# Delta rule on one NeuronCore: the order in which TensorE takes the heads of both parities

## The chip, the cores and the metric

The kernel runs on one core of one Trainium2 chip. The metric is the device time of one execution in microseconds; the median of several runs counts. A profile of one execution gives every instruction's start and length on each engine: TensorE (PE, with its weight loads as PEld), VectorE (DVE), ScalarE (ACT), GpSimd (POOL) and the queue of SyncE that issues transfers (SPq).

## What is computed

The reference is a network of four layers over 256 tokens of width 1024, batch 1. The change concerns one mixer of the third layer, RWKV-7 time mixing, which is a delta rule with 8 heads of dimension 64:

```python
def step(state, inp):                       # state: per head 64 x 64
    r_t, w_t, k_t, v_t, kk_t, b_t = inp
    sa = jnp.einsum('bhvk,bhk->bhv', state, -kk_t)
    state = (state * w_t[:, :, None, :] + sa[..., None] * b_t[:, :, None, :]
             + v_t[..., None] * k_t[:, :, None, :])
    return state, jnp.einsum('bhvk,bhk->bhv', state, r_t)
_, y = lax.scan(step, state0, xs)           # over 256 tokens
...
y = ((y - mu) * lax.rsqrt(var + RW_GN_EPS)).reshape(b, s, c) * lnx_g + lnx_b
y = (y + bonus.reshape(b, s, c)) * g
```

Behind it come the output projection of this layer, its feed-forward part, and a fourth layer with a mixture of experts, which takes the second half of the time.

## The kernel before

**Tiling.** The 256 tokens are taken in two halves of 128 (`tt` = 0, 1), and each half in four chunks of 32 (`cc`, `CH`). The eight heads are four pairs `j`; the head `h = 2j + odd` has parity `odd`. In tensors that lie by feature, an even head has partitions 0 to 63 and an odd one 64 to 127 (`rows_of`), so these are also the rows of TensorE's array that it uses; where the output goes to `rows_of(h)`, the parity also sets the half of the array's columns. All of it is fp32, and PE runs each such product as two instructions, all at the one line of the helper `mm` (L476).

**The stage, on PE** (`delta_pe`, once for each half): transposes to token order (L2123); for each head the products `mp` (L2131, L2132), which VectorE masks (L2288); the lower triangles `low` (L2134 to L2141), four heads of one parity into one PSUM bank, masked by VectorE at L2294; warm-ups (`keep_warm`: products on constants whose result nobody reads); five levels of powers of a triangular inverse; the products NV, WT (L2187, heads in turn) and Z. Then for each chunk: the products `u` with the state (L2201 to L2211), one warm-up ahead of them and one behind, the sums on VectorE (L2327, one for each parity), the products `s` of the new state (L2216 to L2220, heads in turn), and the state's update on VectorE (L2335, L2340). Last the outputs `y` (L2225 to L2239): for each parity a bank, and in it for each head one product with `u`, one with the values (both over 128 tokens into 64 columns), and four with the chunks' states (64 rows into 64 columns).

**Beside it.** `beside(i)` places steps of another attention (MLA) between these, on all engines, and for i = 13 to 17 the normalisation of the first half's y: mean, variance, and `finish_dve` with `affine_act` (L2443 to L2450 on VectorE, L2463 on ScalarE), which stand ahead of the second half's copies in each engine's order.

**What comes behind.** ScalarE copies y from its two banks (L2268), once for each parity; in the first half the token copies (L2247) and the masks of the next half (L2288) wait for the last y. In the second half PE goes on with the output projection (`out_pe`): it first takes the parts that do not need y (k = 4 to 7), with the mean of y behind the first of them (`rest_of_delta`, `mean_pe`), the variance later, and then the parts that need the finished y (L2454 on VectorE). The state products of a half end with the marker that lets `finish_dve` of the first half run.

**Order.** Each engine runs its own list in order, and semaphores join them. PSUM has eight banks, six of which (`short`) are used here in turn; `bank_free` waits for the release of the bank's user six openings before. The weights stream through a ring of slots; SyncE issues a slot's transfers when its last user is done. In this stage no slot comes free and next to nothing is transferred.

Of the kernel before, what the change touches and what calls it, by code (L numbers as in the profile page):

```python
# [23 lines left out]
P = 128  # L24
# [4 lines left out]
HD = 64  # L29
# [15 lines left out]
CH = 32  # L45
# [429 lines left out]
def mm(pe, out, lhsT, rhs, start=True, stop=True):  # L475
    return pe.matmul(out, lhsT, rhs, start=start, stop=stop)  # L476
# [3 lines left out]
def warm(g, pe, ps, count):  # L480

    for _ in range(count):
        mm(pe, ps[:, 0:SHARED], g.tab("mean"), g.tabs[:, 0:SHARED])


def keep_warm(g, pe, count):


    pe.wait_ge(*g.bank_free())
    warm(g, pe, g.psum[g.next_bank("short")], count)  # L490
# [1614 lines left out]
def rows_of(h):  # L2105
    return slice(HD * (h % 2), HD * (h % 2) + HD)


def delta_pe(g, pe, tt, beside):

    pe.wait_ge(g.s["dve_delta"], g.at("A~"))
    pe.wait_ge(g.s["dve_delta"], g.at("shifted", 11))
    pe.wait_ge(g.s["dve_delta"], g.at("B~"))
    pe.wait_ge(g.s["dve_delta"], g.at("K~"))
    pe.wait_ge(g.s["dve_delta"], g.at("R~"))
    pe.wait_ge(g.s["dve_delta"], g.at("chunk ends"))
    c = slice(P * tt, P * tt + P)
    src = [g.ar[:, :, tt, 0, :], g.bt[:, :, c], g.kt[:, :, c], g.prj[:, 8:12, 1 + P * tt:1 + P * tt + P]]
    for n, s in enumerate(src):
        pe.wait_ge(*g.bank_free())  # L2120
        ps = g.open(("tok", tt, n))
        for j in range(4):
            last = pe.transpose(ps[:, P * j:P * j + P], s[:, j, :], g.tab("ident"))  # L2123
        last.then_inc(g.s["pe_delta"], 1)
        g.count("pe_delta", ("mm", "tok", tt, n))
    for h in range(8):
        r, j = rows_of(h), h // 2
        pe.wait_ge(*g.bank_free())
        ps = g.open(("mp", tt, h))
        both = g.ar[r, j, tt, :, :].rearrange("p w c -> p (w c)")  # L2130
        mm(pe, ps[:, 0:256], g.bt[r, j, c], both)  # L2131
        mm(pe, ps[:, 256:512], g.kt[r, j, c], both).then_inc(g.s["pe_delta"], 1)  # L2132
        g.count("pe_delta", ("mm", "mp", tt, h))
    for odd in range(2):  # L2134
        pe.wait_ge(*g.bank_free())
        ps = g.open(("low", tt, odd))
        for j in range(4):
            r = rows_of(odd)
            last = mm(pe, ps[:, P * j:P * j + P], g.ar[r, j, tt, 0, :], g.bt[r, j, c])
        last.then_inc(g.s["pe_delta"], 1)  # L2140
        g.count("pe_delta", ("mm", "low", tt, odd))  # L2141

    keep_warm(g, pe, 4)
    for lv in range(5):
        pe.wait_ge(g.s["dve_delta"], g.at("F", tt, lv, 0))
        pe.wait_ge(g.s["dve_delta"], g.at("F", tt, lv, 1))
        pe.wait_ge(g.s["dve_delta"], g.at("powers", tt, lv, 0))
        pe.wait_ge(g.s["dve_delta"], g.at("powers", tt, lv, 1))
        pe.wait_ge(*g.moment(("lows", tt, lv, 0)))
        pe.wait_ge(*g.moment(("lows", tt, lv, 1)))  # L2150
        for odd in range(2):
            heads = [2 * j + odd for j in range(4)]
            if lv < 4:
                pe.wait_ge(*g.bank_free())
                ps = g.open(("D", tt, lv, odd))
                for j, h in enumerate(heads):
                    last = mm(pe, ps[:, P * j:P * j + P], g.mp[:, h, 0, :], g.dm[:, h, :])
                last.then_inc(g.s["pe_delta"], 1)
                g.count("pe_delta", ("mm", "D", tt, lv, odd))
            if lv < 3:  # L2160
                pe.wait_ge(*g.bank_free())
                ps = g.open(("U", tt, lv, odd))
                for j, h in enumerate(heads):
                    last = mm(pe, ps[:, P * j:P * j + P], g.dm[:, h, :], g.mp[:, h, 0, :])
                last.then_inc(g.s["pe_delta"], 1)
                g.count("pe_delta", ("mm", "U", tt, lv, odd))
            if lv > 0:
                pe.wait_ge(*g.bank_free())
                ps = g.open(("Fp", tt, lv, odd))
                for j, h in enumerate(heads):  # L2170
                    last = mm(pe, ps[:, P * j:P * j + P], g.dm[:, h, :], g.fm[:, h, :])
                last.then_inc(g.s["pe_delta"], 1)
                g.count("pe_delta", ("mm", "Fp", tt, lv, odd))
            g.also("pe_delta", ("read", tt, lv, odd))
        beside(9 * tt + lv)
    pe.wait_ge(g.s["dve_delta"], g.at("F", tt, 5, 0))
    pe.wait_ge(g.s["dve_delta"], g.at("F", tt, 5, 1))
    pe.wait_ge(*g.bank_free())
    ps = g.open(("NV", tt))
    for h in range(8):  # L2180
        last = mm(pe, ps[:, HD * h:HD * h + HD], g.mp[:, h, 2, :], g.tok[:, 3, HD * h:HD * h + HD])
    last.then_inc(g.s["pe_delta"], 1)
    g.count("pe_delta", ("mm", "NV", tt))
    pe.wait_ge(*g.bank_free())
    ps = g.open(("WT", tt))
    for h in range(8):
        last = mm(pe, ps[rows_of(h), P * (h // 2):P * (h // 2) + P], g.tok[:, 0, HD * h:HD * h + HD], g.fm[:, h, :])  # L2187
    last.then_inc(g.s["pe_delta"], 1)
    g.count("pe_delta", ("mm", "WT", tt))
    pe.wait_ge(g.s["act_delta"], g.at("nv", tt))  # L2190
    pe.wait_ge(*g.bank_free())
    ps = g.open(("Z", tt))
    for h in range(8):
        last = mm(pe, ps[:, HD * h:HD * h + HD], g.fm[:, h, :], g.nv[:, HD * h:HD * h + HD])
    last.then_inc(g.s["pe_delta"], 1)
    g.count("pe_delta", ("mm", "Z", tt))
    pe.wait_ge(g.s["act_delta"], g.at("wt", tt))
    for cc in range(4):
        n = 4 * tt + cc
        q = slice(CH * cc, CH * cc + CH)  # L2200
        for odd in range(2):  # L2201
            pe.wait_ge(*g.bank_free())
            ps = g.open(("u", n, odd))
            if odd == 0:
                warm(g, pe, ps, 1)
                pe.wait_ge(g.s["dve_delta"], g.at("state", n))
            for j in range(4):
                last = mm(pe, ps[q, HD * j:HD * j + HD], g.wt[rows_of(odd), j, q],
                          g.states[rows_of(odd), n % 5, HD * j:HD * j + HD])
            last.then_inc(g.s["pe_delta"], 1)  # L2210
            g.count("pe_delta", ("mm", "u", n, odd))  # L2211
        pe.wait_ge(*g.bank_free())
        ps = g.open(("s", n))
        warm(g, pe, ps, 1)
        pe.wait_ge(g.s["dve_delta"], g.at("U row", n))
        for h in range(8):  # L2216
            o = ps[rows_of(h), HD * (h // 2):HD * (h // 2) + HD]
            v = slice(HD * h, HD * h + HD)
            mm(pe, o, g.tok[q, 2, v], g.tok[q, 3, v], True, False)
            last = mm(pe, o, g.tok[q, 1, v], g.u[q, v], False, True)  # L2220
        last.then_inc(g.s["pe_delta"], 1)
        g.count("pe_delta", ("mm", "s", n))
        beside(9 * tt + 5 + cc)

    for odd in range(2):  # L2225
        r = rows_of(odd)
        pe.wait_ge(*g.bank_free())
        ps = g.open(("y", tt, odd))
        for j in range(4):
            h = 2 * j + odd  # L2230
            v, o = slice(HD * h, HD * h + HD), slice(P * j, P * j + P)
            mm(pe, ps[r, o], g.u[:, v], g.mp[:, h, 1, :], True, False)
            mm(pe, ps[r, o], g.tok[:, 3, v], g.mp[:, h, 3, :], False, False)
            for cc in range(4):
                o = slice(P * j + CH * cc, P * j + CH * cc + CH)
                last = mm(pe, ps[r, o], g.states[r, (4 * tt + cc) % 5, HD * j:HD * j + HD],
                          g.ar[r, j, tt, 1, CH * cc:CH * cc + CH], False, cc == 3)
        last.then_inc(g.s["pe_delta"], 1)
        g.count("pe_delta", ("mm", "y", tt, odd))  # L2239


def delta_act(g, act, tt, beside):
# [989 lines left out]
def second_block(g, kind, e):  # L3232
# [18 lines left out]
    for t in range(2):  # L3251
        only("pe", delta_pe, t, beside)
        only("act", delta_act, t, beside)
        only("dve", delta_dve, t, beside)
# [326 lines left out]
```

## Time and profile before

| | |
|---|---|
| median of 3 runs | 2783.79 us (2780.58 to 2784.04) |
| the profiled execution | 2780.89 us, span 2779.1 us, mean granted clock 0.981 |
| PE busy | 2663.9 us, 96% |
| VectorE / ScalarE busy | 1818.8 us, 65% / 1458.3 us, 52% |
| the delta rule | about 1201 to 1357 us of the span |
| y of each half | 1268.6 to 1277.8, 1347.9 to 1357.2 |

The span runs from the first to the last instruction; the execution is 1.8 us longer. A row of the timeline merges neighbours of one kind: it has the start of the first, the time to the end of the last, and the count. Matmuls overlap in the pipeline, so one lasts longer than the distance to the next, and from the length of a group of n the tail of one is taken off before it is divided. "128\*64 128x128" is the part of the array that a matmul uses (rows by columns) and the tile it writes. The clock's column PEclk is 1.00 for 2.4 GHz and 0.50 for 1.2 GHz.

### The profile page before, as it was taken

The page shows a single profiled execution, that of the slowest core. Times are in us where ns is not written, and L with a number is a line of the kernel's source. Part 1 is how long each engine was busy: PE and PEld are TensorE (multiplying, and loading weights), DVE is VectorE, ACT ScalarE, POOL GpSimd, SP SyncE. Part 2 cuts the span into 40 slices and gives each one's busy share as a digit, 9 for nine tenths or more (in the row PEclk, how much of TensorE's full clock was granted, in tenths as well). Part 3 has the DMA queues.
Part 4 walks back from the last instruction along what each step waited for, and adds up shares of the span by engine and source line. Part 5 has one row for each costly group of instructions (what it writes and reads, how often), then busy time and mean ns, then how long its engine had stood idle before and what let it go on. Part 6 is the DMA issues. An engine that isn't in the chain of part 4 may idle for free.

```text
span 2779.1 us, 39065 instructions
## 1 busy us (share of the span) xinstructions
PE 2663.9 (96%) x15510; PEld 2246.9 (81%) x15510; DVE 1818.8 (65%) x1912; ACT 1458.3 (52%) x1624; POOL 29.5 (1%) x40
## 2 busy tenths in 40 slices
PE   6999989999898999899999998899999999999999
PEld 4775678888796999877799996788888888888887
DVE  4224675553534786774454544788888888888887
ACT  3226343342325565522244343677777777777776
POOL 0002000000002000000000000000000000000000
PEclk9999999999999999999999999899999999999999
DMA  8456422222230445320144440799999999999996
GB/s 348 166 213 243 152 91 91 91 107 83 105 131 34 187 173 187 118 92 1 37 174 156 171 182 14 270 365 346 365 341 344 372 346 364 348 369 346 357 360 259
DMA packets 84360, 590.45 MB, mean 212 GB/s; under 512 B 9616, under 2 KB 10000, under 8 KB 19472
## 3 DMA queue, kind: packets, MB, share of 16 engines
q1 hardware_dynamic: 82800, 576.79, 55.6%
q10 hardware_dynamic: 1440, 11.93, 1.1%
q8 instruction: 91, 1.49, 0.2%
q14 instruction: 29, 0.24, 0.0%
HBM read 587.63 MB, written 1.05 MB: 212 GB/s over the span
## 4 chain that ended last, share of the span: by engine, by line
PE 90%; DVE 5%; ACT 3%; issue 1%; DMA 1%; DVEq 0%; POOL 0%; ACTq 0%; POOLq 0%; SPq 0%
PE banks L470 24%; PE banks L472 24%; PE banks L471 24%; PE banks L476 16%; PE banks L2894 1%; PE banks L925 1%; DMA hT<-in_h 1%; DVE rstd L830 0%; DVE ring_rounded L545 0%; DVE aT L2288 0%; ACT scratch L1002 0%; DVE activations L1445 0%; DMA ring<-in_stream 0%; ACT scratch L1015 0%; DVE scratch L2075 0%
## 5 line engine op out<-in xcount | busy, mean ns | idle before, releaser
L471 PE MATMUL banks<-ring_rounded,activations_rounded 128*128 128x512 f32 x1344 | 523.2, 389 | 0.0
L471 PE MATMUL banks<-aT_rounded,ring_rounded 128*128 128x256 f32 (+1 forms) x1096 | 355.8, 325 | 0.0
L472 PE MATMUL banks<-aT_rounded,ring_rounded 128*128 128x256 f32 (+2 forms) x1120 | 336.0, 300 | 0.0
L545 DVE TENSOR_TENSOR ring_rounded<-ring,ring_rounded 128x2048 fp32r<-128x2048 f32 (+4 forms) x112 | 225.4, 2018 | 161.2 <-ACT ring_rounded L535 160.3
L471 PEld LDWEIGHTS banks<-ring_rounded,activations_rounded 128*128 128x128 f32 x1344 | 252.7, 188 | 50.2
L3068 DVE TENSOR_TENSOR ring_rounded<-ring,tables_rounded 128x2048 fp32r<-128x2048 f32 x112 | 253.6, 2288 | 24.1 <-ACT tables_rounded L2986 23.4
L3068 DVE TENSOR_TENSOR ring_rounded<-ring,aT_rounded 128x2048 fp32r<-128x2048 f32 x112 | 254.5, 2286 | 14.5 <-ACT aT_rounded L2986 13.6
L2986 ACT ACTIVATE tables_rounded<-ring 128x2048 fp32r<-128x2048 f32 x112 | 215.0, 1920 | 87.6 <-DMA ring<-in_stream 81.6
L535 ACT ACTIVATE ring_rounded<-ring 128x2048 fp32r<-128x2048 f32 (+4 forms) x112 | 188.5, 1690 | 133.0 <-PE banks L472 99.9
L2986 ACT ACTIVATE aT_rounded<-ring 128x2048 fp32r<-128x2048 f32 x112 | 215.0, 1920 | 71.2 <-DMA ring<-in_stream 58.8
L470 PE MATMUL banks<-aT_rounded,ring_rounded 128*128 128x256 f32 (+1 forms) x776 | 235.0, 303 | 16.6 <-DVE aT_rounded L855 12.5
L472 PE MATMUL banks<-activations_rounded,ring_rounded 128*128 128x512 f32 (+1 forms) x724 | 244.9, 338 | 0.0
L471 PEld LDWEIGHTS banks<-aT_rounded,ring_rounded 128*128 128x128 f32 x1096 | 213.8, 195 | 15.2 <-issue 0.5
L472 PEld LDWEIGHTS banks<-aT_rounded,ring_rounded 128*128 128x128 f32 (+1 forms) x1120 | 218.2, 195 | 5.7
L545 DVE TENSOR_TENSOR ring_rounded<-ring,third_upper_rounded 128x2048 fp32r<-128x2048 f32 (+3 forms) x56 | 113.7, 2030 | 101.1 <-ACT third_upper_rounded L535 100.7
L470 PE MATMUL banks<-tables_rounded,activations_rounded 128*128 128x512 f32 x448 | 176.7, 394 | 0.0
L470 PE MATMUL banks<-aT_rounded,activations_rounded 128*128 128x512 f32 x448 | 176.0, 393 | 0.0
L472 PE MATMUL banks<-tables_rounded,activations_rounded 128*128 128x512 f32 x448 | 174.6, 390 | 0.0
L472 PE MATMUL banks<-aT_rounded,activations_rounded 128*128 128x512 f32 x448 | 174.6, 390 | 0.0
L471 PE MATMUL banks<-aT_rounded,third_upper_rounded 128*128 128x256 f32 (+1 forms) x536 | 173.9, 324 | 0.0
L470 PEld LDWEIGHTS banks<-aT_rounded,ring_rounded 128*128 128x128 f32 x776 | 152.7, 197 | 22.5 <-issue 18.8
L470 PE MATMUL banks<-activations_rounded,ring_rounded 128*128 128x512 f32 (+1 forms) x464 | 157.8, 340 | 0.0
(353 smaller groups left out, 5534.8 us busy)
## 6 DMA issues: line engine op xcount, KB each, us to landing
ring<-in_stream SPq DMA_DIRECT2D x501, 1024.0 KB, 5.5
ring<-in_stream SPq DMA_DIRECT2D x32, 704.0 KB, 5.1
ring<-in_stream SPq DMA_DIRECT2D x28, 768.0 KB, 6.0
activations<-in_rpb ACTq DMA_DIRECT2D x2, 1536.0 KB, 6.2
ring<-in_stream SPq DMA_DIRECT2D x6, 512.0 KB, 5.0
tables<-in_tab_b ACTq DMA_DIRECT2D x1, 2436.0 KB, 8.8
tables<-in_tab_a ACTq DMA_DIRECT2D x1, 2304.0 KB, 13.1
hT<-in_h ACTq DMA_DIRECT2D x1, 2048.0 KB, 15.8
```

Of the source, the lines that this page charges most:

```text
L470: pe.matmul(out, exact(upper), exact(w_upper), start=start, stop=False)
L471: pe.matmul(out, exact(upper), exact(w_lower), start=False, stop=False)
L472: return pe.matmul(out, exact(lower), exact(w_upper), start=False, stop=stop)
L476: return pe.matmul(out, lhsT, rhs, start=start, stop=stop)
L535: act.activation(exact(upper), w, ACT.Copy).then_inc(g.s["act_pieces"], 1)
L545: dve.tensor_tensor(exact(w), w, rounded(upper), ALU.subtract).then_inc(g.s["dve_pieces"], 1)
L925: last = pe.transpose(ps[:, o * w + P * t:o * w + P * t + P], probs[:, j % 2, o, P * t:P * t + P], g.tab("ident"))
L2894: last = pe.transpose(g.psum[4 + q % 2][:, P * j:P * j + P], g.hb[:, q % 2, P * j:P * j + P], g.tab("ident"))
L2986: act.activation(exact(g.upper[u % UPPERS]), g.units[u % EXPERT_RING], ACT.Copy).then_inc(s["act_split"], 1)
L3068: dve.tensor_tensor(exact(w), w, rounded(g.upper[u % UPPERS]), ALU.subtract).then_inc(s["dve_split"], 1)
```

## The change

Three loops of `delta_pe` are turned inside out. The lower triangles, the products u and the outputs y opened a bank for even heads, filled it, signalled, and then did the same for odd heads. Now both banks are waited for and opened first, and each product of an even head is followed by the same product of its odd neighbour. In y this goes term by term: the product with `u` of both, the one with the values of both, then each chunk's state product of both. Both signals of a stage are now given by its last two products. The warm-up ahead of u now stands behind the opening of both banks. The products, their number, operands and banks, the order of accumulation within a head, and all other engines' lists stay as they are.

```diff
--- before.py
+++ after.py
@@ -2131,14 +2131,17 @@
         mm(pe, ps[:, 0:256], g.bt[r, j, c], both)
         mm(pe, ps[:, 256:512], g.kt[r, j, c], both).then_inc(g.s["pe_delta"], 1)
         g.count("pe_delta", ("mm", "mp", tt, h))
+    banks = []
     for odd in range(2):
         pe.wait_ge(*g.bank_free())
-        ps = g.open(("low", tt, odd))
-        for j in range(4):
+        banks.append(g.open(("low", tt, odd)))
+    for j in range(4):
+        for odd in range(2):
             r = rows_of(odd)
-            last = mm(pe, ps[:, P * j:P * j + P], g.ar[r, j, tt, 0, :], g.bt[r, j, c])
-        last.then_inc(g.s["pe_delta"], 1)
-        g.count("pe_delta", ("mm", "low", tt, odd))
+            last = mm(pe, banks[odd][:, P * j:P * j + P], g.ar[r, j, tt, 0, :], g.bt[r, j, c])
+            if j == 3:
+                last.then_inc(g.s["pe_delta"], 1)
+                g.count("pe_delta", ("mm", "low", tt, odd))
 
     keep_warm(g, pe, 4)
     for lv in range(5):
@@ -2198,17 +2201,19 @@
     for cc in range(4):
         n = 4 * tt + cc
         q = slice(CH * cc, CH * cc + CH)
+        banks = []
         for odd in range(2):
             pe.wait_ge(*g.bank_free())
-            ps = g.open(("u", n, odd))
-            if odd == 0:
-                warm(g, pe, ps, 1)
-                pe.wait_ge(g.s["dve_delta"], g.at("state", n))
-            for j in range(4):
-                last = mm(pe, ps[q, HD * j:HD * j + HD], g.wt[rows_of(odd), j, q],
+            banks.append(g.open(("u", n, odd)))
+        warm(g, pe, banks[0], 1)
+        pe.wait_ge(g.s["dve_delta"], g.at("state", n))
+        for j in range(4):
+            for odd in range(2):
+                last = mm(pe, banks[odd][q, HD * j:HD * j + HD], g.wt[rows_of(odd), j, q],
                           g.states[rows_of(odd), n % 5, HD * j:HD * j + HD])
-            last.then_inc(g.s["pe_delta"], 1)
-            g.count("pe_delta", ("mm", "u", n, odd))
+                if j == 3:
+                    last.then_inc(g.s["pe_delta"], 1)
+                    g.count("pe_delta", ("mm", "u", n, odd))
         pe.wait_ge(*g.bank_free())
         ps = g.open(("s", n))
         warm(g, pe, ps, 1)
@@ -2222,21 +2227,27 @@
         g.count("pe_delta", ("mm", "s", n))
         beside(9 * tt + 5 + cc)
 
+    banks = []
     for odd in range(2):
-        r = rows_of(odd)
         pe.wait_ge(*g.bank_free())
-        ps = g.open(("y", tt, odd))
-        for j in range(4):
-            h = 2 * j + odd
-            v, o = slice(HD * h, HD * h + HD), slice(P * j, P * j + P)
-            mm(pe, ps[r, o], g.u[:, v], g.mp[:, h, 1, :], True, False)
-            mm(pe, ps[r, o], g.tok[:, 3, v], g.mp[:, h, 3, :], False, False)
-            for cc in range(4):
-                o = slice(P * j + CH * cc, P * j + CH * cc + CH)
-                last = mm(pe, ps[r, o], g.states[r, (4 * tt + cc) % 5, HD * j:HD * j + HD],
+        banks.append(g.open(("y", tt, odd)))
+    for j in range(4):
+        o = slice(P * j, P * j + P)
+        for term in range(2):
+            for odd in range(2):
+                h = 2 * j + odd
+                v = slice(HD * h, HD * h + HD)
+                x = g.tok[:, 3, v] if term else g.u[:, v]
+                mm(pe, banks[odd][rows_of(odd), o], x, g.mp[:, h, 3 if term else 1, :], term == 0, False)
+        for cc in range(4):
+            o = slice(P * j + CH * cc, P * j + CH * cc + CH)
+            for odd in range(2):
+                r = rows_of(odd)
+                last = mm(pe, banks[odd][r, o], g.states[r, (4 * tt + cc) % 5, HD * j:HD * j + HD],
                           g.ar[r, j, tt, 1, CH * cc:CH * cc + CH], False, cc == 3)
-        last.then_inc(g.s["pe_delta"], 1)
-        g.count("pe_delta", ("mm", "y", tt, odd))
+                if (j, cc) == (3, 3):
+                    last.then_inc(g.s["pe_delta"], 1)
+                    g.count("pe_delta", ("mm", "y", tt, odd))
 
 
 def delta_act(g, act, tt, beside):
```

## Rows read from the trace of the kernel before

**Rows 1.** The page, part 4: the chain that ended last, by engine.

```profile
PE 90%; DVE 5%; ACT 3%; issue 1%; DMA 1%; DVEq 0%; POOL 0%; ACTq 0%; POOLq 0%; SPq 0%
```

**Rows 2.** The chain of waits of the stage: start us, us, what.

```profile
1268.17 9.71 PE banks L476 x104
...
1345.13 41.68 PE banks L476 x278
```

**Rows 3.** Timeline of u and s: start, length (us), engine, line, count, [idle].

```profile
1248.40 0.89 PE L476 MATMUL banks<-scratch,activations 64*32 64x64 f32 x16
1249.14 0.74 DVE L2327 TENSOR_TENSOR activations<-banks,activations 32x256 f32<-32x256 f32 x2 [4.87 <-PE banks L476]
...
1249.21 0.91 PE L476 MATMUL banks<-tables 128*128 128x384 f32 x2
...
1250.06 1.19 PE L476 MATMUL banks<-activations 32*64 32x64 f32 x32
...
1340.83 0.43 DVE L2340 TENSOR_TENSOR scratch<-scratch,chunk_ends 128x256 f32<-128x256 f32 x1
1341.31 0.72 PEld L476 LDWEIGHTS banks<-scratch,activations 64*32 64x32 f32 x16 [0.75 <-DVE scratch L2340]
...
1345.87 0.78 DVE L2327 TENSOR_TENSOR activations<-banks,activations 32x256 f32<-32x256 f32 x2 [0.79 <-PE banks L476]
...
1346.79 1.20 PE L476 MATMUL banks<-activations 32*64 32x64 f32 x32
```

**Rows 4.** Timeline, outputs y of the first half.

```profile
1269.70 0.65 PE L476 MATMUL banks<-aT,activations 128*64 128x128 f32 x4
...
1270.28 0.65 PE L476 MATMUL banks<-activations,scratch 64*64 64x32 f32 x8
...
1277.81 1.96 PE L2123 MATMUL banks<-tables,activations 128*128 128x128 f32 x16
1277.92 0.59 ACT L2268 ACTIVATE activations<-banks 64x512 f32<-64x512 f32 x1 [4.05 <-PE banks L476]
```

**Rows 5.** Timeline, the WT products and the pooling products.

```profile
836.87 1.09 PE L476 MATMUL banks<-scratch,pool_w 64*64 64x256 f32 x8 [0.69 <-ACT scratch L1159]
...
1244.75 1.09 PE L476 MATMUL banks<-scratch,activations 128*64 128x128 f32 x16
```

**Rows 6.** Timeline: masks, lower triangles, warm-ups, first half.

```profile
1204.03 4.88 DVE L2288 TENSOR_TENSOR aT<-banks,tables 128x512 f32<-128x512 f32 x8 [2.74 <-PE banks L476]
...
1207.96 2.85 PE L476 MATMUL banks<-tables 128*128 128x384 f32 x8
1208.83 1.28 DVE L2294 TENSOR_TENSOR scratch<-banks,tables 128x512 f32<-128x512 f32 x2
```

**Rows 7.** Timeline, end of the second half and the output projection.

```profile
1347.91 0.65 PE L476 MATMUL banks<-aT,activations 128*64 128x128 f32 x4
...
1353.05 1.65 ACT L2463 ACTIVATE activations<-activations,vectors 128x128 f32<-128x128 f32 x4 [15.42 <-DVE activations L2446]
...
1354.61 0.57 ACT L2268 ACTIVATE activations<-banks 64x512 f32<-64x512 f32 x1
...
1357.19 1.99 PE L476 MATMUL banks<-hT,ring 128*128 128x256 f32 x8
1357.30 0.59 ACT L2268 ACTIVATE activations<-banks 64x512 f32<-64x512 f32 x1 [2.11 <-PE banks L476]
...
1359.02 1.02 PE L476 MATMUL banks<-activations,tables 128*128 128x512 f32 x2
...
1371.23 1.22 DVE L2454 TENSOR_TENSOR aT<-activations 128x1024 f32<-128x1024 f32 x1
...
1372.82 13.98 PE L476 MATMUL banks<-aT,ring 128*128 128x256 f32 x64
```

**Rows 8.** Two stretches: busy us (count) by engine, PEclk, DMA share.

```profile
1299.00:1302.60 3.60, 1.97 (x19) 1.43 (x18) 2.92 (x7) 1.85 (x4) 0.00 (x0) 1.00 0.00 0
1302.60:1306.00 3.40, 3.40 (x18) 3.40 (x18) 0.26 (x1) 0.00 (x0) 0.00 (x0) 0.50 0.00 0
```

## The prediction

> **What bounds the kernel now.** I read the page first, then the chain of waits around the stage of the delta rule, then the timeline of that stage. The page gives TensorE (PE) 90% of the chain that ended last [rows 1]. In the stage itself the chain is on PE without a break through the two places that the change touches most: the output products of the first half lie in one piece of 9.71 us, those of the second half in one of 41.68 us that runs on into the output projection [rows 2]. So time taken from PE there is taken from the end, unless something that PE then waits for is late. No transfer limits the stage.
>
> **The outputs (y).** One head is six products of fp32, which PE runs as twelve instructions: four that use all 128 rows and 64 columns of the array, then eight on a 64 by 64 quadrant. From the second head on the blocks start 0.58 us apart, and the seven heads from 1269.70 to 1277.81 take 8.11 us, 1.16 us each [rows 4]. Eight heads are 9.27 us; the second half shows the same (1347.91 to 1357.19, 9.28 us) [rows 7]. All heads of one parity use the same half of the columns (and, for the quadrant products, of the rows), so nothing can run side by side. The change puts the twin of the other parity behind each product. What is that worth? Two rows are near. The WT products have exactly the shape and the tiles of the full-height part, and take the heads in turn: 16 instructions in 1.09 us [rows 5]. Less the tail of one (about 0.27) that is 0.055 per instruction, where y's four need 0.58 us for a block, 0.145 each. The pooling product has exactly the diagonal pair of quadrants, each parity into its own bank: 8 instructions of 256 columns in 1.09 us [rows 5], where 8 full-array ones of 256 columns take 1.99 us [rows 7]. And the state products s, alternating in columns, run 32 instructions in 1.19 us, 0.03 each [rows 3], so pairs of short instructions are not held by issue. I therefore take full pairing: two heads in the time of one, 1.16 us. Per half 4 x 1.16 = 4.64 us remain of 9.28, 4.64 us saved. Bounds: the saving cannot be over 4.64 without more than two tiles at once; below, it is the tile-change cost of the slower rival.
>
> Of the full-height four I weigh a rule against this. The rows say that they pair [rows 5]. The Trainium skill ("TensorE: Matmul & The Clock Gate", "The mechanism" in its part on packing) says that a weight load overlaps matmuls in flight only when the row group differs; here only the columns differ, so by it they would not pair. The measured row stands against that, and it gives the rival "quadrants only" below.
>
> **First half (tt = 0): 4.64 us.** Behind y are the transposes of the second half on PE, the copies on ScalarE and the masks on VectorE. ScalarE copied the even output while PE worked on the odd one; now both copies start after y, one after the other, some 0.5 us more than the one copy that followed y before (1277.92, 0.59 us) [rows 4]. They delay the token copies behind them by 0.5 us. Those free banks that the mp products want only later, and the masks start on mp, not on the tokens; PE has some 1.9 us of transposes to run meanwhile [rows 4]. I take 0; without that cover it is at most 0.5.
>
> **Second half (tt = 1): 3.3 us, not 4.64.** Behind y, PE runs eight matmuls of the output projection and then the mean of y, which needs both copies. Before, the mean started at 1359.02 with its copy done at 1357.89 (1357.30 + 0.59) [rows 7]. All 4.64 us earlier it would be at 1354.38. But ScalarE has the four affine steps of the first half before the copies, and they wait for VectorE, not for y: 1353.05 to 1354.70 [rows 7]. The even copy was already ready and started at 1354.61 [rows 7]; the odd one now follows about 0.48 later and ends at 1355.67. The mean starts at about 1355.74, a stall of some 1.4 us. Gain 1359.02 - 1355.74 = 3.28, say 3.2 with the restart. What is late next: the final y arrives at 1372.45 (1371.23 + 1.22), and PE wants it at 1372.82 [rows 7]; both hang on the mean, so this order stays. Bounds 2.7 to 4.64.
>
> **The products with the state (u), eight of them: 1.0 us.** A group of 16 instructions holds PE from 1248.40; one warm-up product follows at 1249.21 and the state products s at 1250.06 [rows 3]. VectorE has both sums done at 1249.88 (1249.14 + 0.74) [rows 3], 0.18 us before; for the last group it is 1346.65 against 1346.79, 0.14 [rows 3]. From a VectorE end to the PE start that waits for it 0.05 us pass (1340.83 + 0.43 to 1341.31) [rows 3]. So s waits for the warm-up, not for VectorE. With pairing (0.03 an instruction, as in s) the group has ended at about 1249.09, before VectorE starts at 1249.14, so VectorE moves not at all, the warm-up ends 0.24 us earlier, and s starts 0.05 behind VectorE: 0.09 to 0.18 us each, eight times, about 1.0. Bounds 0 (the even half comes later, VectorE with it) and 1.9 (8 x 0.24, all of it carried on).
>
> **The lower triangles: 0.** They end before 1207.96, where the warm-ups begin, but VectorE masks mp until 1208.91 (1204.03 + 4.88) and takes the first of them at 1208.83 [rows 6]. PE's gain, at most 0.8 us of 16 instructions, is covered twice: by VectorE and by the warm-ups. The added wait for a second bank (it frees when an early mask is done) stands ahead of the same covered work: 0. If VectorE were faster than PE here it would be worth those 0.8 us. The waits for both banks ahead of u and y find banks freed long before: 0.
>
> **Sum.** 4.64 + 3.2 + 1.0 = 8.9 us. The profiled execution took 2780.89 us, so 2772.0 for it. Its time is the low one of those shown (median 2783.79, 2780.58 to 2784.04); on the median the forecast is 2774.9.
>
> **The clock.** The granted clock fell to the 1.2 GHz level (0.50) from 1302.60 to 1306.00, behind a stretch in which PE was busy for 1.97 of 3.60 us [rows 8]. Where PE is the bound such a stretch costs half its length, 1.7 us. Everything behind y moves by 5 us and PE gets one new stall of 1.4 us; some stretch may come or go. I estimate the spread at two either way, 3.4 us.
>
> **Rivals.** *Quadrants only*: the full-height part does not pair. Then two heads take 2 x 0.58 less one change of form of 0.145 for it, and 0.58 for the quadrants: 1.59 instead of 2.32, 2.9 us saved per half (in the second half nothing then stalls), with u 6.9: 2776.9. For it: nothing in the trace; against: the WT row. *Clock*: three more slow stretches take 5.1 us of the 8.9: 2780.0. For it: three falls are near already; against: denser work. *Tail swallowed*: the second half's y chain is later than I work out, and 3.2 us are lost: 2778.1. *It does nothing*: PE already reaches ahead across parities, as it does a little at the seams. Then 2783.8; against: y's even pace of 0.58 us a block. *Slower*: a change of tile costs what a change of form costs. A block of four lasts 0.58 where paired work needs 4 x 0.11 = 0.44, so 0.14 for a change. There are now 12 tile changes for each pair of heads, 48 a half, 96 in all, and 64 in u: 160 x 0.14 = 22 us, 2806. It decides once a change costs over 0.097 us (4.64 / 48). Against: WT, s and pooling change tiles all the time at full pace.
>
> **How the numbers follow.** Forecast 0.62, clock 0.18, quadrants only 0.07, slower 0.05, tail 0.05, nothing 0.03. The range 2769 to 2781 takes in the forecast with its clock spread, the two partial rivals and the clock rival, and leaves out slower, nothing and the ends of the clock: under 2 in 10. About 0.2% (5.6 us, below 2778.2) is what a measurement of this kernel can tell from no change. Faster: 0.62 + 0.06 + 0.02 + 0.03 = 0.73. Slower 0.05. The same 0.22.
>
> **What the profile after would show.** y holds PE for about 4.64 us a half, its two copies directly behind each other; the mean waits on ScalarE for over 1 us behind eight matmuls of the projection; s starts 0.05 us behind VectorE; masks and lower triangles on VectorE as before. Wrong would be: full-height blocks that still take 0.58 us for each parity; masks that do not move up with y; more time at the lower clock.

## The result and the profile after

The changed kernel takes 2764.61 us (median of 4 runs, 2761.59 to 2765.47) beside 2783.91 us for the kernel before (2780.58 to 2784.91): ratio 0.9931, 95% interval 0.9914 to 0.9948. It is 19.3 us faster, where 8.9 us were forecast, and lies below the range. The profiled execution took 2763.85 us, span 2762.1 us, 17.0 us less than the one before. Of all executions in this document one, of e6_before_plus2, lies far outside the others (6985.7 us, at a granted clock of 1.00); it moves that kernel's median by 0.1 us.

The page's chain has hardly changed in kind; PE's share is two points lower.

```profile
PE 88%; DVE 6%; ACT 3%; DMA 1%; issue 1%; POOL 0%; ACTq 0%; DVEq 0%; POOLq 0%; SPq 0%
```

The timeline of y in the first half, of the changed kernel (start, length, engine, line, tile, count), answers to [rows 4]:

```profile
1270.33 0.61 PE L476 MATMUL banks<-aT,activations 128*64 128x128 f32 x8
...
1271.45 0.66 PE L476 MATMUL banks<-aT,activations 128*64 128x128 f32 x8
...
1272.04 0.66 PE L476 MATMUL banks<-activations,scratch 64*64 64x32 f32 x16
...
1274.97 1.97 PE L2123 MATMUL banks<-tables,activations 128*128 128x128 f32 x16
1275.07 1.21 ACT L2279 ACTIVATE activations<-banks 64x512 f32<-64x512 f32 x2 [2.78 <-PE banks L476]
```

A block has twice the instructions (8 and 16) and takes as long, 0.58 or 0.59 us from one to the next. From the start of y at 1270.33 to the transposes at 1274.97 it is 4.64 us. Both copies stand in one row now, directly behind y. The pairing is complete, in the full-height part too.

The end of the second half, which answers to [rows 7]:

```profile
1341.45 0.66 PE L476 MATMUL banks<-aT,activations 128*64 128x128 f32 x8
...
1346.14 1.99 PE L476 MATMUL banks<-hT,ring 128*128 128x256 f32 x8
1346.59 1.65 ACT L2474 ACTIVATE activations<-activations,vectors 128x128 f32<-128x128 f32 x4 [15.11 <-DVE activations L2457]
...
1348.14 1.19 ACT L2279 ACTIVATE activations<-banks 64x512 f32<-64x512 f32 x2
...
1349.38 1.12 PE L476 MATMUL banks<-activations,tables 128*128 128x512 f32 x2 [1.25 <-ACT activations L2279]
...
1361.70 1.23 DVE L2465 TENSOR_TENSOR aT<-activations 128x1024 f32<-128x1024 f32 x1
...
1363.29 2.97 PE L476 MATMUL banks<-aT,ring 128*128 128x256 f32 x13
```

y lasts 4.69 us here (1341.45 to 1346.14). Then PE runs its eight matmuls and waits 1.25 us for ScalarE's copies, which stand behind the affine steps. The finished y (1361.70 + 1.23) still comes before PE's late part of the output projection (1363.29), so this order has stayed as it was.

One product u with its neighbours, twice; these answer to [rows 3]:

```profile
1266.22 0.64 PE L476 MATMUL banks<-scratch,activations 64*32 64x64 f32 x16
...
1266.89 0.78 DVE L2338 TENSOR_TENSOR activations<-banks,activations 32x256 f32<-32x256 f32 x2 [0.39 <-PE banks L476]
...
1267.01 0.91 PE L476 MATMUL banks<-tables 128*128 128x384 f32 x2 [0.16 <-ACT ring L1002]
...
1267.86 1.19 PE L476 MATMUL banks<-activations 32*64 32x64 f32 x32
...
1339.32 0.91 PE L476 MATMUL banks<-tables 128*128 128x384 f32 x2
1339.49 0.77 DVE L2338 TENSOR_TENSOR activations<-banks,activations 32x256 f32<-32x256 f32 x2 [0.79 <-PE banks L476]
...
1340.32 1.19 PE L476 MATMUL banks<-activations 32*64 32x64 f32 x32
```

In the second of them the warm-up follows u at once and s starts 0.06 us behind VectorE (1339.49 + 0.77). In the first one the warm-up waits for ScalarE, which still uses its bank, and s comes as late as before but for 0.02 us. The latter happens in two of the eight.

That is all that the pairing does to instructions. The rest goes with the clock. The same five stretches of work, from the first mask of the second half to the start of the experts, first in the kernel before, then after (stretch; length, busy time and count of PE, PEld, DVE, ACT, POOL; PEclk; DMA share; GB/s):

```profile
1280.94:1333.74 52.80, 45.67 (x334) 38.54 (x331) 22.25 (x41) 10.63 (x22) 0.00 (x0) 0.90 0.00 1
1333.74:1360.08 26.34, 26.07 (x302) 18.63 (x300) 11.64 (x23) 3.97 (x8) 0.00 (x0) 1.00 0.00 1
1360.08:1407.08 47.00, 43.03 (x230) 38.59 (x229) 27.26 (x43) 17.94 (x32) 0.00 (x0) 0.93 0.24 90
1407.08:1607.10 200.02, 195.61 (x1597) 194.26 (x1596) 103.96 (x113) 86.68 (x103) 0.00 (x0) 0.98 0.46 167
1607.10:1791.61 184.51, 169.16 (x986) 138.97 (x985) 99.47 (x190) 84.37 (x153) 0.00 (x0) 0.94 0.39 143
```

```profile
1278.10:1327.70 49.60, 42.30 (x335) 35.68 (x333) 22.24 (x41) 10.90 (x23) 0.00 (x0) 0.97 0.01 1
1327.70:1350.55 22.85, 21.05 (x299) 13.90 (x300) 11.64 (x23) 3.97 (x8) 0.00 (x0) 1.00 0.01 1
1350.55:1396.50 45.95, 41.98 (x230) 37.54 (x229) 27.25 (x44) 17.94 (x32) 0.00 (x0) 0.96 0.25 92
1396.50:1596.08 199.58, 195.18 (x1597) 193.82 (x1596) 103.89 (x112) 86.66 (x103) 0.00 (x0) 0.98 0.46 168
1596.08:1776.45 180.37, 164.70 (x986) 136.62 (x985) 99.33 (x190) 85.62 (x153) 0.00 (x0) 0.96 0.39 147
```

Up to the first of them the changed kernel gained 4.92 us (it had come into the stage 2.08 us late, since its profile has 58.0 us at 1.2 GHz ahead of 1281 us where that of before has 47.8, and reached the mask 2.84 us early). The second stretch is 3.49 us shorter, with the clock at 1.00 in both: that is u (0.43) and y (3.06). The third, fourth and fifth contain none of the changed products; the first has the lower triangles, worth nothing by e3 below, and the first group of u, whose gain comes only behind its end at VectorE's start. Yet they are 3.20, 1.05, 0.44 and 4.14 us shorter, each with a higher granted clock or the same rounded one. 1.8 us more come behind the fifth. In this pair of executions 8.4 us are direct, 8.8 us come with the clock within the five stretches and 1.8 us behind them, and 2.1 us had been lost ahead of the stage: 17.0 in all, but for rounding. The time at 1.2 GHz within the stretches fell from 47.8 to 27.3 us; half of the difference, which is what it costs where TensorE is the bound, is 10.2 us.

### The profile page after: what moved, and what is told of

It is laid out like the page before. It is cut to its first block, busy times and chain, and to the rows that moved or that the text cites. A ratio compares the mean times of both kernels' runs of the same rounds, so it can differ in the third digit from the quotient of the medians.

```text
span 2762.1 us, 39075 instructions
## 1 busy us (share of the span) xinstructions
PE 2643.7 (96%) x15510; PEld 2229.4 (81%) x15510; DVE 1817.5 (66%) x1912; ACT 1457.8 (53%) x1624; POOL 29.4 (1%) x40
## 3 DMA queue, kind: packets, MB, share of 16 engines
HBM read 587.63 MB, written 1.05 MB: 213 GB/s over the span
## 4 chain that ended last, share of the span: by engine, by line
PE 88%; DVE 6%; ACT 3%; DMA 1%; issue 1%; POOL 0%; ACTq 0%; DVEq 0%; POOLq 0%; SPq 0%
PE banks L470 24%; PE banks L472 24%; PE banks L471 24%; PE banks L476 15%; PE banks L2905 1%; DMA ring<-in_stream 1%; PE banks L925 1%; DMA hT<-in_h 1%; DVE rstd L830 0%; DVE ring_rounded L545 0%; DVE aT L2299 0%; ACT scratch L1002 0%; DVE activations L1445 0%; ACT scratch L1015 0%; DVE nmax L968 0%
```

## The experiments

"Direct" below is the part of a kernel's gain that its timeline shows up to the copy of y, outside places where the clock differs; "slow time" is the time at the 1.2 GHz level between about 1281 and 1792 us of the span, summed from the granted clock of the profile. A "fall" is a change of the granted clock from 2.4 to 1.2 GHz, and a slow stretch is the time until it rises again. Each time is compared with the kernel before on the same chip.

### One part at a time

**e1_y_only** has the new y with the old u and lower triangles, **e2_u_only** the new u alone, **e3_low_only** the new lower triangles alone; each is the hunk of the diff above that its name says.

> Only the outputs y take the parities in turn; u and the lower triangles as before. The change as a whole gave 19.3 us, of which the traces of before and after show some 8 as time taken from TensorE in y and 1 in u, and the rest spread over places where the granted clock falls. Theory A (the clock gain comes from y's pairing or from the earlier time behind it): 17 to 18.5 us faster than before. Theory B (u is what keeps the clock up, because TensorE waits between u and s eight times): 8 us faster, the rest comes with u.

> Only u takes the parities in turn. Theory A: 1.0 us faster (s starts 0.05 us behind VectorE instead of 0.14 to 0.24), at most 1.5. Theory B: about 10 us faster, the clock falls less often.

> Only the lower triangles take the parities in turn. Both theories: 0 within 1 us, since VectorE is still masking; this also shows how far a kernel with another instruction order and no gain of its own scatters. If it is faster by 5 us or more, the lower triangles carry what I cannot place.

Measured: y alone 2767.71 us (ratio 0.9952, 0.9938 to 0.9966), u alone 2775.97 us (0.9972, 0.9963 to 0.9981), the lower triangles alone 2782.83 us (1.0003, 0.9994 to 1.0012), beside 2782.91 us. The lower triangles are worth nothing, as forecast. But u is worth 6.9 us and y 15.2 us: neither theory has it so, and the sum, 22.1, is more than the 19.3 of both. Directly, u's profile shows 0.34 us in the first half and 0.43 in the second, y's 4.58 and 3.06. The first of the five stretches in u's profile:

```profile
1282.27:1331.87 49.60, 42.46 (x335) 36.19 (x333) 22.25 (x40) 10.64 (x22) 0.00 (x0) 0.97 0.01 1
```

It is 49.60 us long as after the change, at the same clock of 0.97, though only 0.34 us have been won ahead of it.

### The time put back

**e4_filled** is the change with filler work behind y:

```diff
+    keep_warm(g, pe, 7)        # at the end of delta_pe, behind y, in each half
```

> The whole change, with seven warm-up products (4.5 us of TensorE) behind y of each half, so that TensorE goes on at the time at which it did before. Theory C (the earlier time and not the pairing sets where the clock falls): all but u's 1 us and its share is gone, 2782 to 2784. Theory D (the denser work itself keeps the clock up): the direct 8 us are gone and the clock gain of some 10 us stays, 2772 to 2774.

Measured: 2774.84 us (0.9975, 0.9966 to 0.9984). By the numbers this is nearest to theory D. But its timeline is that of e2_u_only: the filler gives y's time back to within 0.1 us, some 0.8 us stay (u's 0.77 and a rest of the filler), and the slow time is the same 34.1 us in both, in stretches at the same places of the program. So y's pairing by itself, without the time that it saves, shows no effect on the clock. Otherwise it tells what e2 does: a third of a microsecond ahead of the second half goes with 7 us less in all. Whether the pairing of u does that or the shift is open after it.

### The kernel before, only later

**e5_before_plus1**, **e6_before_plus2** and **e7_before_plus3** pair nothing. They add work:

```diff
     pe.wait_ge(g.s["dve_delta"], g.at("chunk ends"))
+    if tt == 1:
+        keep_warm(g, pe, 1)    # 2 and 3 in the other two
     c = slice(P * tt, P * tt + P)
```

> The kernel before, with one warm-up product (0.64 us of TensorE) ahead of the second half's transposes. The profiles so far show the order of the u products taking 0.8 us directly and, behind a shift of 0.3 us, two slow-clock stretches of three less at 1300 to 1326. Theory P (a small shift in time, whatever makes it, decides which gaps of TensorE the clock falls behind): the kernel does more work, yet comes out faster than before by 2 us or more, here or in one of the next two runs. Theory Q (the pairing of u itself keeps the clock): 0.6 us slower, the same stretches at the low clock.

> As the run before with two warm-up products (1.28 us). Theory P: as there, the slow stretches of the second half differ in number from before's three. Theory Q: 1.3 us slower, three slow stretches between 1300 and 1330.

> As the run before with three warm-up products (1.92 us). Theory P: as there. Theory Q: 1.9 us slower, three slow stretches between 1300 and 1330.

Measured: 2775.98 us (0.9978, 0.9968 to 0.9988), 2781.13 us (0.9996, 0.9986 to 1.0006) and 2778.48 us (0.9992, 0.9982 to 1.0002), beside 2781.92 us. The added work costs 0.70, 1.34 and 2.01 us directly, yet the first is 5.9 us faster than the kernel before. The other two can't be told from it (both intervals hold 1), and e6's time alone would not rule out Q. The clock does: of the three slow stretches between 1300 and 1330 us that Q keeps, e5 and e6 have none and e7 has one. Theory P stands, Q falls. The same instructions of TensorE as in [rows 8], in e5_before_plus1:

```profile
1301.60:1305.20 3.60, 1.97 (x19) 1.43 (x18) 2.91 (x7) 1.85 (x4) 0.00 (x0) 1.00 0.00 0
1305.20:1308.60 3.40, 3.40 (x33) 3.40 (x33) 0.26 (x1) 0.00 (x0) 0.00 (x0) 1.00 0.00 0
```

PE was busy for the same 1.97 of 3.60 us before. There the clock fell and PE got through 18 instructions in the next 3.40 us; here it stayed at 1.00 and PE got through 33. By the time of the span all this comes 2.6 us later, but 1.9 us of that had been lost ahead of the stage and the clock's own changes had moved with it. The last slow stretch ahead of the stage, in the kernel before and in e5_before_plus1:

```profile
1121.67:1128.50 6.83, 5.25 (x24) 5.28 (x25) 6.56 (x18) 4.16 (x9) 0.00 (x0) 0.50 0.01 2
1123.53:1130.35 6.82, 5.22 (x24) 5.25 (x25) 6.55 (x18) 4.16 (x9) 0.00 (x0) 0.50 0.02 8
```

From its end to the first mask of the first half it is 75.5 us in the one (1128.50 to 1204.03) and 75.6 in the other (1130.35 to 1205.94), and 75.2 to 75.6 in all fourteen profiles, though that mask stands anywhere from 1204.0 to 1207.0 us. So what differs against this clock is the 0.70 us of added work. Kernels whose work stands at the same place have their slow stretches at the same place: those of e3_low_only are those of the kernel before, each 1.0 to 1.1 us later, as all of its work is, and counted from the end of that earlier stretch all nine begin at the same time to 0.1 us.

### Which instructions pair

**e8_quadrants_only** changes the order inside the new y:

```diff
-        for term in range(2):
-            for odd in range(2):
+        for odd in range(2):
+            for term in range(2):
                 h = 2 * j + odd
```

> The change, but in y the four full-height instructions of a head stay together (even, then odd), and only the quadrant products alternate. If the full-height part pairs by columns, as the timeline after suggests, y takes 1.7 us more in each half than after the change (4.64 - 2.9). If only row groups pair, as the rival had it, y lasts the same as after the change. If alternation inside the full-height part is not needed because TensorE looks ahead over four instructions, it also lasts the same, and the length of y alone tells pairing from none: 4.7 us a half means paired, 6.4 us not.

The timeline of its y:

```profile
1269.42 0.66 PE L476 MATMUL banks<-aT,activations 128*64 128x128 f32 x8
...
1270.59 0.67 PE L476 MATMUL banks<-aT,activations 128*64 128x128 f32 x8
...
1271.18 0.65 PE L476 MATMUL banks<-activations,scratch 64*64 64x32 f32 x16
...
1274.13 1.97 PE L2123 MATMUL banks<-tables,activations 128*128 128x128 f32 x16
```

The full-height blocks, now four instructions of one parity and then four of the other, are as short as alternating ones, and y takes 4.71 us (1269.42 to 1274.13). So it is paired all the same, where only the columns differ; pairing does not need neighbours, it reaches over at least four instructions. The rival "quadrants only" is out; the full-height blocks of the change, eight instructions in 0.66 us, had already spoken against it. The kernel takes 2768.76 us (0.9956, 0.9939 to 0.9972): 13.2 us less than before, where the change has 19.3, with nearly the same direct gain (8.3 us) and 44.4 us of slow time against 27.3.

### The changed kernel at other places in time, and without the stall

**e9_after_plus1** and **e10_after_plus2** add the same warm-up products to the changed kernel. **e11_copies_first** moves ScalarE's copies of the second half ahead of the affine steps, **e12_copies_first_plus1** does both:

```diff
-    for cc in range(4):
+    for cc in range(4 - tt):
         beside(9 * tt + 5 + cc)
...
     g.also("act_delta", ("y done", tt))
+    if tt:
+        beside(17)
```

> The changed kernel with one warm-up product (0.64 us) ahead of the second half's transposes. Theory P says that before stood badly (three slow stretches in the second half) and after stands about as well as others: directly 0.64 us slower than after, with slow stretches that may differ by one or two either way, so 2762 to 2769. Theory R (the changed kernel keeps the clock by itself, wherever it stands): 2765.2, 0.64 us over after, the same slow stretches.

> The changed kernel with two warm-up products (1.28 us) there. Theory P: 2762 to 2770, slow stretches at other places than after's or in another number. Theory R: 2765.9, the same slow stretches.

> The changed kernel, with ScalarE's two copies of y of the second half ahead of the four affine steps of the first half. If the stall of TensorE ahead of the mean is what cost the second half 1.5 us of its 4.6, the mean starts directly behind eight matmuls again, and the output projection's late part comes up to 1.3 us earlier than after the change; the slow-clock stretches behind it may take or add 2 us. If the copies are not what the mean waits for, the timeline up to there stays.

> As the run before, with one warm-up product (0.64 us) ahead of the second half's transposes: the direct gain of the copies, up to 1.3 us, once more at another place in time. Compared with the changed kernel plus one warm-up product it should be 1.0 to 1.3 us less up to the output projection; beyond that the slow stretches decide.

Measured: 2770.79 us (0.9958, 0.9941 to 0.9975), 2774.18 us (0.9966, 0.9952 to 0.998), 2770.43 us (0.9955, 0.9939 to 0.9972) and 2771.09 us (0.9955, 0.9938 to 0.9971), beside 2783.22 us. Beside before these gain 12.4 and 9.0 us, where the change gains 19.3: adding 0.7 and 1.3 us of work to the changed kernel costs some 7 and 10 us. The interval of e9 still overlaps that of the change (0.9914 to 0.9948) a little, that of e10 does not; and the slow stretches stand at other places in both, which R rules out. R falls. Both times are over P's upper ends, 2769 and 2770, since I took it for granted that the changed kernel stands about as well as others, and it stands best. e11's timeline:

```profile
1345.88 1.99 PE L476 MATMUL banks<-hT,ring 128*128 128x256 f32 x8
1345.98 1.21 ACT L2279 ACTIVATE activations<-banks 64x512 f32<-64x512 f32 x2 [14.77 <-PE banks L476]
1347.22 1.65 ACT L2476 ACTIVATE activations<-activations,vectors 128x128 f32<-128x128 f32 x4
...
1347.71 1.02 PE L476 MATMUL banks<-activations,tables 128*128 128x512 f32 x2
```

The copies start with the eight matmuls, and the mean follows these without a stall: 1.83 us behind their start (1345.88 to 1347.71) instead of 3.24 (1346.14 to 1349.38). Up to the output projection's late part the gain is 1.52 us (1.3 were expected), which is all that the second half's 3.06 lack of the first half's 4.58, so the cause of that loss is shown. Still the kernel gains 6 to 7 us less than the change (12.8 beside 19.3; the intervals overlap a little), and its profile has 41.0 us of slow time against 27.3. The same holds with one warm-up more: e12 reaches the late part 1.52 us sooner behind its y than e9, a little over the 1.0 to 1.3 expected, and in the end takes as long (2771.09 beside 2770.79 us; 37.5 us of slow time beside 34.1). By these profiles a better order of work gave its gain away by where it came to stand.

### All of them side by side

| kernel | direct, us | slow time, us | direct + half of slow time less before's | measured against before |
|---|---|---|---|---|
| before | 0 | 47.8 | 0 | 0 |
| after | -8.4 | 27.3 | -18.7 | -19.3 |
| e1 y only | -7.6 | 34.1 | -14.5 | -15.2 |
| e2 u only | -0.8 | 34.1 | -7.6 | -6.9 |
| e3 low only | 0 | 47.8 | 0 | -0.1 |
| e4 filled | -0.9 | 34.1 | -7.7 | -8.1 |
| e5, e6, e7 before + 1, 2, 3 | 0.7, 1.3, 2.0 | 30.7, 37.5, 37.5 | -7.8, -3.8, -3.1 | -5.9, -0.8, -3.4 |
| e8 quadrants only | -8.3 | 44.4 | -10.0 | -13.2 |
| e9, e10 after + 1, 2 | -7.7, -7.1 | 34.1, 41.0 | -14.5, -10.5 | -12.4, -9.0 |
| e11, e12 copies first, + 1 | -9.9, -9.2 | 41.0, 37.5 | -13.3, -14.4 | -12.8, -12.1 |

For e11 and e12 the direct gain is counted up to the late part of the output projection. The slow time is that of one profiled execution, the measured number a difference of medians. Two terms, the direct one and half of the slow time, meet eleven of the thirteen changed kernels within 2.3 us and all within 3.2 us; differences of that size between rows are not explained here. For e8 the profiled execution was the slowest of its four runs (2773.88 us: 8.0 less than before's median there, where the row says 10.0).

## Why the prediction was wrong, point by point

- **The outputs, 4.64 us in the first half:** right; 4.92 with u's 0.34, so 4.58 (e1 shows 4.58 by itself). The two copies behind each other delay the token copies; the gain in PE's time is carried whole to the first mask.
- **The second half, 3.2 us:** right, 3.06; the stall is 1.25 us, it is ScalarE's affine steps that make it, and e11 takes it away.
- **u, 1.0 us:** 0.77. VectorE did not move, as forecast. The step that failed in part: I had s limited by the warm-up's length alone; in two of eight the warm-up waits for a bank that ScalarE still holds.
- **The lower triangles, 0:** right, e3 (0.1 us, within its interval). **The rule on row groups:** the rows had it right. Full-height products of two column halves run side by side, here in y as in WT before; the Trainium skill ("TensorE: Matmul & The Clock Gate", "The mechanism") has weight loads overlap only with another row group, and the measurement decides.
- **The sum, 8.9 us:** its three terms add up to 8.84; the direct gain measured is 8.4.
- **The clock, "two stretches either way, 3.4 us":** this is the step that failed. The mechanism was named, with its price of half a stretch, and it was under-sized by a factor of three and given no sign: the sum had it at nothing, and the runs show some 10 us (half of 20.5 us less at 1.2 GHz, and 10.9 us of the 19.3 that are not direct). I counted two stretches at random around a mean of nothing. In fact the kernel before stood at the worst place of the fourteen (47.8 us of slow time, as e3 has, with three falls in the second half alone; the change has the least, 27.3), so a shift could hardly make it worse. That was to be seen in part: the second half had three falls behind its gaps and the first half, with the same levels, had none. I read one of them as a price and did not add up the others, and the two stretches left no room for the gaps behind the stage, while every one of them, to the start of the experts, was open to it. That the change landed at the best place of all is luck: e9, with 0.7 us more work, gains 4.7 us beyond its direct part, where the change gains 10.9.
- **The range** should have reached down by half of that slow time, not by 3.4 us. The rivals "clock" (worse), "tail", "quadrants only" and "slower" did not occur; a fifth, that the clock gets better by as much as the change itself gives, was missing.

## What to carry to other kernels

Products that use different row or column parts of TensorE's array ran here in pairs at the full pace of each, also when several of one part come before those of the other; look for long runs of products on the same part. The gain ends where the next engine's list has older work ahead of the copy that everybody waits for. When a kernel has gaps that the clock falls behind, sum its time at the lower level before you forecast: a fraction of a microsecond ahead was worth several here (0.70 us of added work made e5 5.9 us faster), so a single comparison of two kernels does not tell an edit's worth; add a little filler at one place to see how much of a difference is position.

## What was not expected of the hardware

Whether the clock falls behind a gap of TensorE's work depends on when the gap comes: the same gap (1.97 us busy of 3.60) was followed by the 1.2 GHz level in one kernel and by 2.4 GHz in another that comes to it with 0.70 us more work behind it. The places are not random from run to run: in all fourteen profiles the stage begins 75.2 to 75.6 us behind the end of the same slow stretch, kernels with the same work ahead have the same falls, the four runs of the changed kernel lie within 3.9 us, at mean granted clocks of 0.984 or 0.985, and the eight of the kernel before beside e9 too (2781.8 to 2785.73). They are not wholly fixed either: the 24 beside e5 to e8 spread over 11.9 us (2776.74 to 2788.63). What fixes them to the program is open; no run here moved them apart from moving the work, so a forecast of where a given shift lands is not to be had from these runs. How far the part of the gain that comes behind the start of the experts (1.8 us in the profiled pair) belongs to it is open too: the time from there to the end is between 984.6 and 990.5 us in the fourteen profiles.
